# A mixture-of-experts stage in plain fp32: projections without splits, paired 64-column tiles, a ring of 35 weight blocks

## What is computed

```python
def swiglu(h, w_gate, w_up, w_down):
    return (jax.nn.silu(h @ w_gate) * (h @ w_up)) @ w_down

D_EXPERT = D_MODEL // 2          # 512
N_EXPERTS = 32; TOP_K = 2
```

## Time and profile before

| | us |
|---|---|
| median of 3 runs | 2100.73 |
| lowest, highest | 2100.49, 2109.09 |
| span of the profiled execution | 2107.8 |
| time that lies nearest to that span | 2109.09 |

### The profile page before, as it was taken

The page is one execution under the profiler, slowest core; times in us unless marked ns, Lnnn a source line. Parts: engine busy times, 40 slices in busy tenths (PEclk is TensorE's granted clock), DMA queues, the critical chain, the costliest instruction groups (busy, mean ns, idle before and its releaser), DMA issues.

```text
span 2107.8 us, 23713 instructions
## 1 busy us (share of the span) xinstructions
PE 2036.5 (97%) x9256; PEld 1576.7 (75%) x9256; DVE 1371.9 (65%) x1899; ACT 1076.8 (51%) x1569; POOL 153.7 (7%) x115
## 2 busy tenths in 40 slices
PE   8999999989999889999999999999989999999998
PEld 6888887856878668888888887776776666776665
DVE  5443544476666866544344465657789898999997
ACT  5222223354445454423122344645678888888884
POOL 0000000000000001000000000000012112222230
PEclk9999999999899899999999999999989999999999
DMA  6433333347444114333333332211459999999997
GB/s 199 146 98 104 93 100 76 81 62 70 56 62 82 60 38 142 100 92 99 92 100 99 90 100 70 60 50 46 170 180 400 398 397 398 401 400 397 394 396 275
DMA packets 289720, 351.69 MB, mean 167 GB/s; under 512 B 14768, under 2 KB 228784, under 8 KB 289600
## 3 DMA queue, kind: packets, MB, share of 16 engines
q1 hardware_dynamic: 280080, 326.43, 49.0%
q0 software_dynamic: 9520, 23.66, 3.1%
HBM read 337.71 MB, written 20.45 MB: 170 GB/s over the span
## 4 chain that ended last, share of the span: by engine, by line
PE 87%; DVE 8%; ACT 3%; issue 1%; DMA 0%; SPq 0%; DVEq 0%; ACTq 0%
PE bank L181 86%; PE bank L184 2%; ACT p L187 1%; DVE PTL L193 1%; DVE y L193 0%; ACT wH L187 0%; DVE score L199 0%; DVE p L196 0%; DVE st L205 0%; DVE score L217 0%; DVE gt L193 0%; DMA stage<-w_gate 0%; ACT T L187 0%; DVE olL L193 0%; ACT rr L187 0%
## 5 line engine op out<-in xcount | busy, mean ns | idle before, releaser
L181 PE MATMUL bank<-hH,wH 128*128 128x512 f32 x1104 | 444.5, 403 | 11.6 <-DVE stage0L L193 9.6
L181 PE MATMUL bank<-hL,wH 128*128 128x512 f32 x1104 | 437.1, 396 | 0.0
L187 ACT ACTIVATE wH<-stage 128x1024 fp32r<-128x1024 f32 (+3 forms) x284 | 283.4, 1007 | 108.5 <-PE bank L181 84.7
L181 PEld LDWEIGHTS bank<-hH,wH 128*128 128x128 f32 x1104 | 212.6, 193 | 61.0 <-DVE stage0L L193 9.6
L181 PEld LDWEIGHTS bank<-hL,wH 128*128 128x128 f32 x1104 | 212.6, 193 | 45.7 <-issue 1.9
L187 ACT ACTIVATE w_moe<-stage_moe 128x1024 fp32r<-128x1024 f32 x196 | 203.1, 1054 | 23.6 <-DMA stage_moe<-w_gate 11.4
L181 PE MATMUL bank<-w_moe,xS 128*128 128x512 f32 x374 | 151.1, 404 | 0.0
L181 PE MATMUL bank<-hidH,wH 128*128 128x512 f32 x352 | 137.4, 390 | 2.1 <-DVE stage3L L193 0.9
L181 PE MATMUL bank<-hidL,wH 128*128 128x512 f32 x352 | 137.0, 389 | 0.0
L187 ACT ACTIVATE hidH<-hf 128x512 fp32r<-128x512 f32 x44 | 27.8, 632 | 188.8 <-DVE hf L193 188.8
L226 POOL DMA_INDIRECT pair_results<-yo,pair x30 | 82.6, 2755 | 377.2 <-PE bank L181 339.1
(11 more groups left out here) (586 smaller groups left out, 4637.3 us busy)
## 6 DMA issues: line engine op xcount, KB each, us to landing
stage_moe<-w_down SPq DMA_DIRECT2D x92, 512.0 KB, 12.3
stage<-w_up SPq DMA_DIRECT2D x88, 512.0 KB, 8.3
stage_moe<-w_gate SPq DMA_DIRECT2D x88, 512.0 KB, 11.7
stage<-w_gate SPq DMA_DIRECT2D x84, 512.0 KB, 6.0
stage_moe<-w_up SPq DMA_DIRECT2D x84, 512.0 KB, 12.9
stage<-w_in SPq DMA_DIRECT2D x58, 512.0 KB, 4.5
stage<-w_down SPq DMA_DIRECT2D x52, 512.0 KB, 10.8
pair_results<-zero POOLq DMA_DIRECT2D x8, 512.0 KB, 2.9
```

Source lines behind the costliest of these rows:

```text
L181: return self.e.matmul(*a, **k) if self.e is not None else Nothing()
L187: return self.e.activation(*a, **k) if self.e is not None else Nothing()
```

## The change

- Weight blocks are no longer split: no rounding on ACT, no remainder on DVE, and all products are plain fp32 matmuls on whole blocks (`u.F`). Blocks are loaded alternately from gate and up.
- `project` writes gate to partitions 0 to 63 of a bank and up to partitions 64 to 127 of the same bank, both with the same 64 columns of tokens as the stationary operand: two 128x64 tiles of the array, alternating. `down` does the same with the two halves of its 1024 columns.
- xS has 64 columns instead of 128 and needs no DVE; gate and up are copied by one ACT operation; `turn_hid` has four transposes instead of 16 matmuls; the splits of the hidden values (`split_hid`) and the steps `presplit` are gone.
- The memory that is freed becomes 19 more tiles of the ring, 35 in all. They are appended behind the 16, with the event from which each may be written: six from the router's matmul, one from the norm factors, four from the last transposes of the rows, one from the transposes of x, four from the last store of token rows, three from the event `ei`.
- The second half of yo is now copied by DVE for every expert, the last one too, after ACT's half.

```diff
-            M.hS = [pair([128, 3, BLK], "hS") for _ in range(2)]
...
-            M.xS = [sb([128, 8, 2 * BLK], F32R, "xS") for _ in range(2)]
-            M.gu = [[sb([128, 512], F32, name) for _ in range(2)] for name in ("gS", "uS")]
+            M.xS = [sb([128, 8, BLK], F32, "xS") for _ in range(2)]
+            M.gu = [sb([128, 512], F32, "gu") for _ in range(2)]
...
-                highs.slots.append([sb([128, 1024], F32R, "w_moe"), done, NSPLIT + k])
...
+            def more_tiles(at, end, done):
+                while at + 4096 <= end:
+                    t = nc.alloc_sbuf_tensor_at(f"stage_late{len(stages.slots)}", [128, 1024], F32, offset=at)
+                    stages.slots.append([(t, None), done, len(stages.slots)])
+                    at += 4096
+
+            more_tiles(rest_h, x_place + 49152, ("mm", "router"))
+            more_tiles(high_place, high_place + 4096 * NSPLIT, ("mm", "router"))
+            more_tiles(top_end, top_end + 6144, ("mm", "factors"))
+            more_tiles(mark3, mark3 + 16384, ("mm", "hb", 3, 1))
+            more_tiles(rest_x, x_place + 16384, ("mm", "xt", 3, 1))
+            more_tiles(mark3 + 16384, mark3 + 32768, ("h_rows", 3))
+            more_tiles(mark3 + 32768, moe_top, ("ei",))
...
                     elif s.kind == "project":
+
                         pe.wait_ge(*after("xT", n))
                         if s.i == 0:
                             free(s.bank)
-                        for e, u in enumerate(s.units):
-                            pe.wait_ge(*after("w_lo", u.i))
+                        for e, both_units in enumerate(s.units):
                             kk = 2 * s.i + e
+                            for u in both_units:
+                                pe.wait_ge(*after("land%d" % u.raw.at, u.i))
                             for j in range(2):
-                                x = xS[n % 2][:, 2 * kk + j, :]
-                                pe.matmul(s.bank.t[:, :], x, u.H[:, j, :], start=kk == 0 and j == 0, stop=False)
-                                t = pe.matmul(s.bank.t[:, :], x, u.L[:, j, :], start=False, stop=kk == 3 and j == 1)
-                            t.then_inc(*did("mm", "gu", n, s.k, kk))
+                                for j2, u in enumerate(both_units):
+                                    t = pe.matmul(s.bank.t[BLK * j2:BLK * j2 + BLK, :], xS[n % 2][:, 2 * kk + j, :], u.F[:, j, :],
+                                                  start=kk == 0 and j == 0, stop=kk == 3 and j == 1)
+                            t.then_inc(*did("mm", "project", n, kk))
...
                         for j, u in enumerate(s.units):
-                            if u.whole:
-                                pe.wait_ge(*after("land%d" % u.raw.at, u.i))
-                            else:
-                                pe.wait_ge(*after("w_lo", u.i))
+                            pe.wait_ge(*after("land%d" % u.raw.at, u.i))
                             for c in range(2):
-                                if j == 0:
-                                    free(s.banks[c])
-                                o, at = s.banks[c].t[0:BLK, :], slice(512 * c, 512 * c + 512)
-                                if u.whole:
-                                    t = pe.matmul(o, hF[n % 2][:, j * BLK:j * BLK + BLK], u.F[:, 0, at], start=False, stop=j == 3)
-                                else:
-                                    t = mm3(o, [y[:, j, :] for y in hS[n % 2]], (u.H[:, 0, at], u.L[:, 0, at]), j == 0, False)
-                                t.then_inc(*did("mm", "dn", n, j, c))
+                                t = pe.matmul(s.bank.t[BLK * c:BLK * c + BLK, :], hF[n % 2][:, j * BLK:j * BLK + BLK], u.F[:, 0, 512 * c:512 * c + 512],
+                                              start=j == 0, stop=j == 3)
+                            t.then_inc(*did("mm", "dn", n, j))
...
                     elif s.kind == "down":
-                        for u in s.units:
-                            weights_for(u)
...
-                        if n != NB - 1:
-                            dve.wait_ge(*after("mm", "dn", n, 3, 1))
-                            dve.tensor_copy(rows_of_block(n)[:, 512:1024], s.banks[1].t[0:BLK, :]).then_inc(*did("yo", n, 1))
+                        dve.wait_ge(*after("mm", "dn", n, 3))
+                        dve.wait_ge(*after("yo", n, 0))
+                        dve.tensor_copy(rows_of_block(n)[:, 512:1024], s.bank.t[BLK:2 * BLK, :]).then_inc(*did("yo", n, 1))
```

More of the change, by code:

```diff
@@ L1347, in moe, with project @@
             both_banks = {}
-            def project(n, j2, part):
-                name = ("w_gate_2", "w_up_2")[j2]
+            def project(n, part):
                 if part == 0:
-                    both_banks[n, j2] = banks.take((("gcopy", "ucopy")[j2], n))
-                s = Step("project", n=n, k=j2, i=part, bank=both_banks[n, j2])
-                s.units = [unit([(0, source(n)(name, 2 * kk, 2))], 2, 512, ("mm", "gu", n, j2, kk)) for kk in (2 * part, 2 * part + 1)]
+                    both_banks[n] = banks.take(("gu", n))
+                s = Step("project", n=n, i=part, bank=both_banks[n])
+                s.units = []
+                for kk in (2 * part, 2 * part + 1):
+                    s.units.append([unit([(0, source(n)(name, 2 * kk, 2))], 2, 512, ("mm", "project", n, kk), True) for name in ("w_gate_2", "w_up_2")])
                 add(s)
@@ L1361, in down @@
             def down(n):
-                s = Step("down", n=n)
-                s.banks = [banks.take(("yo", n, c)) for c in range(2)]
-                s.units = [unit([(0, source(n)("w_down_2", j, 1))], 1, 1024, ("mm", "dn", n, j, 1), j == 3) for j in range(4)]
+                s = Step("down", n=n, bank=banks.take(("yo", n, 1)))
+                s.units = [unit([(0, source(n)("w_down_2", j, 1))], 1, 1024, ("mm", "dn", n, j), True) for j in range(4)]
                 add(s)
@@ L1369, in moe @@
             add(Step("wtable", bank=banks.take(("ws",))))
-            add(Step("presplit", i=len(units) + 7, low=len(units) + 5))
             turn_x(0)
-            add(Step("presplit", i=len(units) + 7, low=len(units) + 7))
             turn_x(1)
             add(Step("extras"))
-            for j2 in range(2):
-                for part in range(2):
-                    project(0, j2, part)
+            for part in range(2):
+                project(0, part)
             def spread(n):
@@ L1390, in moe @@
                 if n + 1 < NB:
-                    project(n + 1, 0, 0)
-                    project(n + 1, 0, 1)
+                    project(n + 1, 0)
                 turn_hid(n)
                 if n + 1 < NB:
[L1395 to L1398, removed]
+                    project(n + 1, 1)
                 if n + 2 < NB:
@@ L1417, in moe @@
                 turn_x(n)
-                for j2 in range(2):
-                    for part in range(2):
-                        project(n, j2, part)
+                for part in range(2):
+                    project(n, part)
                 turn_hid(n)
-                add(Step("split_hid", n=n))
                 down(n)
@@ L1782, in expert_steps @@
                     elif s.kind == "turn_hid":
-                        pe.wait_ge(*after("gcopy", n))
-                        pe.wait_ge(*after("ucopy", n))
+                        pe.wait_ge(*after("gu", n))
                         free(s.bank)
[L1787 to L1790, removed]
+                        for j in range(4):
+                            t = pe.transpose(s.bank.t[:, 128 * j:128 * j + 128], M3.gu[n % 2][:, 128 * j:128 * j + 128], mat("ident"))
@@ L1791, in expert_steps @@
                         t.then_inc(*did("mm", "turn_hid", n))
                     elif s.kind == "down":
-                        pe.wait_ge(*after("hS", n))
+                        pe.wait_ge(*after("mhid", n))
+                        free(s.bank)
                         for j, u in enumerate(s.units):
-                            if u.whole:
-                                pe.wait_ge(*after("land%d" % u.raw.at, u.i))
-                            else:
-                                pe.wait_ge(*after("w_lo", u.i))
+                            pe.wait_ge(*after("land%d" % u.raw.at, u.i))
@@ L1876, in moe_stage @@
                     elif s.kind == "fold":
-                        pe.wait_ge(*after("fold",))
                         pe.wait_ge(*after("bd",))
@@ L2308, in expert_steps @@
                         table("silu")
[L2309 to L2314 removed]
+                        act.activation(M3.sg[n % 2][:, :].rearrange("p (k n) -> p k n", k=4),
+                                       s.bank.t[:, :].rearrange("p (k n) -> p k n", k=4)[:, :, 0:BLK], ACT.Silu).then_inc(*did("msilu", n))
                     elif s.kind == "down":
[L2316 to L2317 removed]
                         if n >= NB:
```

57 lines of the change are left out of this document (14 added, 43 removed).

## The result

| | kernel before | changed kernel |
|---|---|---|
| median of the comparison | 2103.46 us | 2093.62 us (5 runs, 2086.99 to 2097.05) |
| ratio, 95% interval | 1 | 0.9936 [0.9915, 0.9957] |
| span of the profiled execution | 2107.8 us | 2095.3 us |
| from the router's first acc matmul to the end | 2107.8 - 1538.8 = 569.0 | 2095.3 - 1548.6 = 546.7 |
| start of that matmul | 1538.8 | 1548.6 |

Faster by 10 to 13 us, where 30 were forecast. The table's last two rows split the miss at the acc matmuls, the last work that the change leaves alone (1538.81 in the earlier trace rows). Behind them 22.3 us were gained instead of 30. Ahead of them, in code that the change does not edit, 9.8 us were lost.

A forecast was written before the change was run, and what follows sets the result against it. PE and the DMA engines were taken to bind the experts' stage at one pace, with a 28 us hole in the block queue before it. Last landing 2055 plus 23 gave 2078, -30 us, so 2071 us from the median; range 2046 to 2098.

The forecast's parts named there:

- a lighter TensorE alone: Experts' stage: PE and the DMA engines run at the same pace, so less PE work moves the steady pace hardly at all.
- Column-tile pairs: Experts' project and down: two matmuls on column tiles run together at full overlap, 12.7 us of PE per expert.
- A: Experts' matmuls: the pairs don't run together, 23.8 us per expert, time 2340 us; chance 0.09.
- B: Experts' matmuls: weight loads no longer hidden; with two exposed per step 19.1 us per expert, time 2190 us; chance 0.05.
- C: Experts' stage: PE has short gaps and its clock drops to 1.2 GHz for half the experts, +136 us; chance 0.04.
- The steady pace: Experts' stage: the DMA engines set 16.62 us per expert, 1.385 us per weight block.
- the ring's: Start of the experts' stage: 19 more tiles keep the block queue running from 1540; last block lands by 2055, -26 us.
- The tail: From the last block's landing to the end: 23 us instead of 26.6, -4 us.
- If the rows' stores and the first gathers take some us longer beside the blocks ... it costs nothing.: Start of the experts' stage: a later first matmul costs nothing, as PE has 30 blocks in hand and needs 12.7 us per 12.
- the sum: Whole kernel: 2055 + 23 = 2078 against the span of 2107.8, -30 us, taken from the median 2100.7: 2071 us.
- allowance of 5 us at the start: Block queue from 1540: 5 us for 2 MB of token rows sharing the engines and what the 16th block still needs.
- D: Start of the experts' stage: the early start brings nothing, 1.396 us per block from 1567, only 4 us won, 2097; chance 0.06.

## Why the prediction was right and where it failed

**Right.** TensorE and the DMA engines ran at one pace, and a lighter TensorE alone moves nothing: with the old ring the ratio was 1.0017. Column-tile pairs run at full overlap: 12.2 us per expert for 12.7, and without overlap 19.07 us. Rivals A and B fall with that. C falls too: the clock stands at 0.98 to 1.00 in the windows of 100 us, though TensorE is busy only 77 of 100. The steady pace was 16.55 us per expert for 16.62. The gain is mostly the ring's, as said (15.5 us). The tail was 22.8 us (2095.3 less 2072.5, the last block's landing) for 23.

**Failed, 1: "If the rows' stores and the first gathers take some us longer beside the blocks ... it costs nothing."** The step counted TensorE's reserve and forgot the queue's, and the sum's allowance of 5 us at the start was too small for it. All 35 tiles are full by then, and only the first expert's matmuls free one. Its projections began 34.0 us after acc instead of 26.7, and SP stood without a tile from 1574.8 to 1585.7. Windows of 4 us from there, 28 to 36 us after acc:

```profile
1576.60:1580.60 4.00, 0.52 (x5) 0.52 (x5) 0.00 (x0) 0.00 (x0) 0.00 (x0) 0.50 1.04 300
1580.60:1584.60 4.00, 3.72 (x20) 2.15 (x20) 0.00 (x0) 1.19 (x2) 0.92 (x1) 0.50 1.02 314
```

With 306 GB/s in the next 4 us and 373 over the following 10, against 400, that is 2.8 + 0.7 = 3.5 us of missing traffic. Four us right behind acc moved at 183 GB/s, worth 2.2 us more. The granted clock is at 0.50 in both rows, the 1.2 GHz level; TensorE had stood idle for 10.12 us ahead of the first transposes. The first project took 4.84 us for its first 16 records instead of 3.6, and freed its tiles the later for it. D was therefore true in part. The last block landed 523.9 us after acc, where 2055 - 1538.8 = 516.2 was forecast: 7.7 us late. Behind acc the gain is 569.0 - 549.5 = 19.5 us (the median of the eight profiles with unaltered experts), two thirds of the 30. The 5.7 us are worked out from windows; no run takes the hole away alone. Over the whole 60 us behind acc, 21.8 MB were moved in this profile and 20.9 MB in the second one of the same kernel, where 400 GB/s would make 24: 5.5 and 7.8 us of traffic are missing. The second one's stretch to the end is longer by 2.4 us (549.1 for 546.7), which fits. Of what lies between these figures and the miss of 7.7 to 10.5 us (549.5 - 539.0), no run splits the rest.

**Failed, 2: what was not a step at all.** The sum took the 1540 us ahead of the router as given. In the eight profiles without TensorE filler that have the new experts, acc starts at 1541.1 to 1548.6, median 1545.3; with the kernel before, three times at 1538.7 to 1539.8. That is some 6 us lost, 9.8 in the profile shown first. Filler that never runs puts it at 1533.6 to 1542.1, which gives between half of the 6 us and more than all of it back. So about a third of the miss (6 of 17 to 20 us) goes with the length of TensorE's program, as far as a few profiles with wander in them can say; by which mechanism stays open.

The difference was taken from the median 2100.7, and the median of the comparison was 2103.5; the range, 2046 to 2098, held the time because it had room for D.

## What to carry to other kernels

Where two resources run at one pace, ask which of them has a hole at the start and fill that: 19 tiles at the right moment were worth 15.5 us, and the lighter TensorE without them nothing. In a ring, cover on the consumer's side is no cover on the queue's: once the ring is full, a late first consumer leaves the queue without a tile. Blocks that are issued ahead of the stores and gathers on which the first consumer waits are what makes it late. When code that an edit does not touch gets slower, look at where the chains part, and try some hundred to some thousand instructions in a block that never runs before explaining the loss by the edit.

## What the runs showed that was not expected

- The length of TensorE's program moves the time of code far ahead of the edit. Without filler the `w_k` load issued at 374.9 lands in 10.0 us and TensorE stands still near 380; with 1504 unexecuted matmuls it is 4.5 us, as in the kernel before. Filler on ScalarE and VectorE alone leaves it at 10.0.
- The same division shows in the DMA engines' busy share from 500 to 600 us, at much the same traffic. It is 0.26 in all eight profiles of the new experts without TensorE filler, and 0.46 to 0.62 in the kernel before and with filler. So more than one load differs. First the kernel before, then the changed one:

```profile
500.00:600.00 100.00, 96.50 (x415) 78.26 (x414) 58.50 (x108) 49.01 (x63) 2.73 (x5) 0.86 0.52 63
```

```profile
500.00:600.00 100.00, 94.55 (x401) 76.02 (x399) 59.19 (x107) 45.37 (x59) 2.73 (x5) 0.86 0.26 65
```

- Two plain fp32 matmuls of 512 columns on column tiles of 64, sharing all 128 rows, cost what one costs: 16 records in 3.60 us, and 7.03 us when both go to the same columns. Each record has a weight load of 0.138 us, and the loads add nothing that shows. The Trainium skill's page "TensorE: Matmul & The Clock Gate" (Part 3, Packing small matmuls) has weight loads overlap running matmuls only between different row groups; here they are hidden although all tiles share the same rows, and the measurement decides.
- Stores of 0.5 MB on POOL's queue, issued behind eleven blocks on SP's, land in 14.5 us. With seven blocks ahead of them it is 11.3, and with none 5.4.
